# Eight modulation rows moved ahead of the routing, and a new order for the last expert group, in an attention and mixture-of-experts layer

## The reference, cut to what matters

```
mod = silu(c) @ w_ada + b_ada                     # 2048 x 12288, six parts: sh1 sc1 g1 sh2 sc2 g2
h = rmsnorm(x, norm1_g) * (1 + sc1) + sh1;  qkv = h @ w_qkv
y = two attentions (sliding window, blockwise), each normalised;  x = x + g1 * (y @ w_o)
h = rmsnorm(x, norm2_g) * (1 + sc2) + sh2
gates = routing(h)                                # group by softmax, two experts of eight in it
for e in range(32):                               # w_gate, w_up: 2048 x 512;  w_down: 512 x 2048
    out += gates[:, e] * ((silu(h @ w_gate[e]) * (h @ w_up[e])) @ w_down[e])
x = x + g2 * out;  return rmsnorm(x, final_g)     # 256 tokens of 2048
```

## Time and profile before

| | |
|---|---|
| median of 3 runs | 1431.66 us (1430.23 to 1432.35) |
| the profiled execution | 1430.98 us, its span 1429.1 us |
| PE | 1311.6 us busy, 92% |
| DVE | 681.7 us, 48% |
| ACT, POOL | 158.0 us, 62.1 us |
| read from memory | 566.27 MB, 398 GB/s over the span |

### The profile page before, as it was taken

The page is one execution under the profiler, slowest core; times in us unless marked ns, Lnnn a source line. Parts: engine busy times, 40 slices in busy tenths (PEclk is TensorE's granted clock), DMA queues, the critical chain, the costliest instruction groups (busy, mean ns, idle before and its releaser), DMA issues.

```text
span 1429.1 us, 14957 instructions
## 1 busy us (share of the span) xinstructions
PE 1311.6 (92%) x5797; PEld 663.2 (46%) x5797; DVE 681.7 (48%) x1069; ACT 158.0 (11%) x424; POOL 62.1 (4%) x74
## 2 busy tenths in 40 slices
PE   4999999999999999999997998989899799888896
PEld 4686688577888635333332332333233233223332
DVE  5678788699987621432332331333233232232235
ACT  3300000295001302000000000000000000000002
POOL 1000000013000100000000000000000000000000
PEclk9999999999999999999999999999999999999999
DMA  9999999983999999999999999999999999999995
GB/s 337 394 396 387 399 401 392 392 287 117 397 400 422 354 426 425 425 425 423 427 427 427 425 425 427 423 430 425 425 427 427 427 425 425 428 425 428 423 425 206
DMA packets 102961, 569.11 MB, mean 398 GB/s; under 512 B 5216, under 2 KB 19808, under 8 KB 70272
## 3 DMA queue, kind: packets, MB, share of 16 engines
q1 hardware_dynamic: 102384, 567.67, 97.5%
q0 software_dynamic: 528, 0.78, 0.4%
HBM read 566.27 MB, written 2.16 MB: 398 GB/s over the span
## 4 chain that ended last, share of the span: by engine, by line
PE 68%; DMA 26%; DVE 2%; ACT 2%; issue 1%; SPq 1%; DVEq 0%; ACTq 0%
DMA ring<-in_w_up 25%; PE PS L1731 22%; PE PS L1490 12%; PE PS L1695 8%; PE PS L1784 6%; PE PS L1596 6%; PE PS L1493 4%; PE PS L1568 2%; DMA ring<-in_w_ada 1%; PE PS L1678 1%; PE PS L1657 1%; PE PS L1716 1%; PE PS L1517 1%; PE PS L1431 0%; PE PS L1746 0%
## 5 line engine op out<-in xcount | busy, mean ns | idle before, releaser
L1731 PE MATMUL PS<-ring,gysq 128*64 128x512 f32 x960 | 222.7, 619 | 40.6 <-DMA ring<-in_w_up 40.6
L1731 PE MATMUL PS<-ring,W 128*64 128x512 f32 x1024 | 236.7, 620 | 21.4 <-DMA ring<-in_w_up 21.4
L939 DVE SCALAR_TENSOR_TENSOR W<-ring,sm,W 128x1024 f32<-128x1024 f32 (+1 forms) x195 | 234.4, 1202 | 21.7 <-DMA ring<-in_w_ada 5.7
L1784 PE MATMUL PS<-ring,W 128*64 128x512 f32 x992 | 219.7, 595 | 12.4 <-ACT W L864 12.4
L1267 DVE TENSOR_TENSOR r<-r,PS 128x512 f32<-128x512 f32 x120 | 82.5, 687 | 232.2 <-PE PS L1695 232.2
L1490 PE MATMUL PS<-r,ring 128*128 128x256 f32 x768 | 167.2, 379 | 0.7 <-DVE r L978 0.7
L1731 PEld LDWEIGHTS PS<-ring,gysq 128*64 128x64 f32 x960 | 79.3, 143 | 183.2 <-issue 183.2
L1490 PEld LDWEIGHTS PS<-r,ring 128*128 128x128 f32 x768 | 145.7, 190 | 22.9 <-issue 3.4
L1731 PEld LDWEIGHTS PS<-ring,W 128*64 128x64 f32 x1024 | 76.6, 142 | 170.2 <-issue 170.2
L1272 DVE TENSOR_SCALAR W<-W 128x256 f32<-128x256 f32 x32 | 21.0, 658 | 280.4 <-ACT W L860 279.6
L1784 PEld LDWEIGHTS PS<-ring,W 128*64 128x64 f32 x992 | 69.4, 137 | 142.3 <-issue 134.4
(11 more groups left out here) (273 smaller groups left out, 833.7 us busy)
## 6 DMA issues: line engine op xcount, KB each, us to landing
ring<-in_w_gate SPq DMA_DIRECT2D x64, 2048.0 KB, 25.5
ring<-in_w_up SPq DMA_DIRECT2D x64, 2048.0 KB, 28.0
ring<-in_w_down SPq DMA_DIRECT2D x64, 2048.0 KB, 28.4
ring<-in_w_ada SPq DMA_DIRECT2D x32, 2048.0 KB, 18.1
ring<-in_w_ada SPq DMA_DIRECT2D x32, 1024.0 KB, 16.2
ring<-in_w_qkv SPq DMA_DIRECT2D x9, 2048.0 KB, 19.0
ring<-in_w_o SPq DMA_DIRECT2D x8, 2048.0 KB, 17.6
ring<-in_w_qkv SPq DMA_DIRECT2D x8, 1536.0 KB, 16.9
```

Source lines behind the costliest of these rows:

```text
L939: ins = V.scalar_tensor_tensor(total, w, cT[:, t:t + 1], total, ALU.mult, ALU.add)
L1731: last = mm(PS[64 * j:64 * j + 64, i % 2, :].rearrange("p (m n) -> p m n", m=2), hE[i % 2][:, k], w[:, :, t, 256 * j:256 * j + 256], start ...
L1784: last = mm(PS[64 * q:64 * q + 64, bank + i2, :], hidT[:, b, 64 * j:64 * j + 64], w[:, b, 512 * ch:512 * ch + 512], start=(j + b == 0), st ...
```

## The change

Three things are changed together.

- The last two chunks of M7 are loaded right after its first two, before any expert chunk, so that all expert chunks m = 0 to 7 stand in eight different slots. The eight last rows on DVE go into WO_ROWS, which now adds up to 64: one more before residual(4), (6), (8), (10) and (12), and three before residual(15).
- The last group of experts has an order of its own, LAST_GROUP: down of expert 1 comes before gate and up of expert 2. On PE the first scatter follows down(1); between the halves of gate_up(3) stand hid_transpose(2) and six keep_warm products; hid_transpose(3) stands between the chunks of down(2), and its result goes to a buffer of its own (hidT_last).
- The last expert's down weights come in four pieces of 512 columns (1 MB each), each with its own signal. All four pieces are multiplied into partitions 64 to 127, one after the other, each into its own bank, and scaled by one DVE instruction each. The last scatter goes through the first token half and then through the second, and ACT computes the first half's root before the last square.

```diff
-TAIL = [(0, 0), (0, 1), (1, 0), (1, 1), (0, 2), (0, 3), (1, 2), (1, 3)]
+LAST_GROUP = ([(0, k) for k in range(4)] + [(1, k) for k in range(4)] + [(0, 4), (0, 5), (1, 4), (1, 5)]
+              + [(2, k) for k in range(4)] + [(3, k) for k in range(4)] + [(2, 4), (2, 5), (3, 4), (3, 5)])
+LAST_GU_AT = [LAST_GROUP.index((i, 0)) for i in range(4)]
+LAST_DN_AT = [LAST_GROUP.index((i, 4)) for i in range(4)]
+TAIL = [(h, ch) for h in range(2) for ch in range(4)]
 TAIL_BANK = [6, 7, 4, 5]
...
+    rows(LAST, 2, 3)
     first = sum(o[2] is not None for o in order) % RING
-    for k in (2, 3):
-        order.append(("rows", (LAST, k), (first + 4 + k) % RING, "rows", ROW_NO[LAST, 4 * k + 3]))
...
+        hidT_last = idr[:, :].rearrange("p (b n) -> p b n", b=2)
...
-        WO_ROWS = [[2, 2, 2, 2], [12, 2, 1, 1], [12, 2, 1, 1], [14, 1, 1, 0]]
+        WO_ROWS = [[2, 2, 2, 2], [13, 2, 2, 1], [13, 2, 2, 1], [15, 1, 1, 3]]
...
+            def last_down(ch, s):
+
+                n0 = D * (ch % 2)
+                return (slot(s)[:, n0:n0 + D].rearrange("p (t n) -> p t n", n=512), down_v[E - 1, :, :, 512 * ch:512 * ch + 512])
...
-                i, k = GROUP[m % 24]
+                i, k = (GROUP if m < EXP_CHUNKS * E - 24 else LAST_GROUP)[m % 24]
                 e = 4 * (m // 24) + i
                 if e == E - 1 and k >= 4:
-                    dst, src = last_down(k - 4, (S0 + m) % RING)
+                    dst, src = last_down(2 * (k - 4), (S0 + m) % RING)
+                    sp.dma_start(dst, src).then_inc(piece_in[k - 4], 16)
+                    dst, src = last_down(2 * (k - 4) + 1, (S0 + m) % RING)
                 else:
                     dst, src = expert_chunk(e, k, (S0 + m) % RING)
...
-                if (kind, i) == ("rows", (LAST, 2)):
-                    for m in range(6):
-                        expert_load(m)
...
-            for m in range(6, EXP_CHUNKS * E):
+            for m in range(EXP_CHUNKS * E):
                 expert_load(m)
...
-                    free = GU_END[i - 2] if i > 1 else GU_END[i + 2] - 24
+                    free = GU_END[i - 2] if i > 1 else max(GU_END[i + 2], LAST_GU_AT[i + 2] + 4) - 24
...
+                if tail:
+                    hidT_evac(1)
+                    exp_gate(2)
+                    selT_evac(2 * q + 1)
+                    hidT_evac(2)
+                    exp_gate(3)
+                    hidT_evac(3)
+                    return
...
-            last_root(0)
+                if k == 6:
+                    last_root(0)
             last_root(1)
...
+            def last_result(ch):
+
+                if ch % 2 == 0:
+                    dve.wait_ge(piece_ps, ch // 2 + 1)
+                else:
+                    dve.wait_ge(pe_chunk, PE0 + EXP_CHUNKS * E - 1 + ch // 2)
+                n0 = 512 * ch
+                V.tensor_tensor(yd[64:128, n0:n0 + 512], PS[64:128, ch, :], g2b[64:128, n0:n0 + 512],
+                                ALU.mult).then_inc(yd_ok, 1)
...
-            for _ in range(8):
-                row()
...
-                silu_up(q, 2)
-                result(q, 1)
+                if not tail:
+                    silu_up(q, 2)
+                result(q, 1, tail)
                 acc_add(2 * q)
+                if tail:
+                    silu_up(q, 2)
...
                 if tail:
-                    last_result(0)
-                    last_result(1)
+                    for ch in range(4):
+                        last_result(ch)
...
-                dve.wait_ge(f_ms, (6, 8)[h])
+                dve.wait_ge(f_ms, 4 * h + 4)
...
-                for j in range(2):
-                    w = slot(chunk_at(g, DN_AT[3] + j)).rearrange("p (b n) -> p b n", b=4)
-                    for b in range(4):
-                        for q in range(2):
-                            last = mm(PS[64 * q:64 * q + 64, j, :], hidT[:, b % 2, 64 * (b // 2):64 * (b // 2) + 64],
-                                      w[:, b, 512 * q:512 * q + 512], start=(b == 0), stop=(b == 3))
-                    last.then_inc(pe_chunk, 1)
                 p = 2 * g + 1
                 pe.wait_ge(selT_ok, p + 1)
+                for ch in range(4):
+                    if ch % 2 == 0:
+                        s = (S0 + LAST_DN_AT[3] + ch // 2) % RING
+                        pe.wait_ge(piece_in[ch // 2], 16)
+                    else:
+                        s = chunk_at(g, LAST_DN_AT[3] + ch // 2)
+                    w = slot(s)[:, D * (ch % 2):D * (ch % 2) + D].rearrange("p (b n) -> p b n", b=4)
+                    for b in range(4):
+                        last = mm(PS[64:128, ch, :], hidT_last[:, b % 2, 64 * (b // 2):64 * (b // 2) + 64], w[:, b],
+                                  start=(b == 0), stop=(b == 3))
+                    last.then_inc((piece_ps, pe_chunk)[ch % 2], 1)
                 for k, (h, ch) in enumerate(TAIL):
-                    if k % 4 == 0:
-                        pe.wait_ge(yd_ok, 4 * p + 4 + k // 2)
+                    if k < 4:
+                        pe.wait_ge(yd_ok, 4 * p + 3 + k)
...
+                        if j == 0 and between:
+                            between()
 
                 pe.wait_ge(sel_ok, 2 * n + 2)
                 sel_transpose(2 * g, 0)
                 gate_up(g, 1)
                 hid_transpose(0)
                 down(0)
+                if tail:
+                    hid_transpose(1)
+                    down(1)
+                    scatter(2 * g, more)
+                    gate_up(g, 2, tail=True)
+                    sel_transpose(2 * g + 1, 1)
+
+                    def third_transpose():
+                        hid_transpose(2)
+                        keep_warm(4, 6)
+
+                    gate_up(g, 3, third_transpose, tail=True)
+                    down(2, lambda: hid_transpose(3))
+                    last_expert()
+                    return
...
-                if tail:
-                    first_scatter()
-                    gate_up(g, 3)
-                else:
-                    gate_up(g, 3, first_scatter)
+                gate_up(g, 3, first_scatter)
```

More of the change, by code:

```diff
@@ L392, in layer_kernel @@
         landed = [sem(f"landed{s}") for s in range(RING)]
+        piece_in, piece_ps = [sem(f"piece_in{i}") for i in range(2)], sem("piece_ps")
         upper_in, late_in = sem("upper_in"), sem("late_in")
@@ L852, in selT_evac, with expert_group @@
                 A.activation(selT, PS[:, 2, 0:T], ACT.Copy).then_inc(selT_ok, 1)
-            def expert_group(q, rest=False):
+            def expert_group(q, rest=False, tail=False):
                 def exp_gate(i):
-                    act.wait_ge(pe_chunk, PE0 + 24 * q + GU_END[i])
+                    act.wait_ge(pe_chunk, PE0 + 24 * q + (LAST_GU_AT[i] + 4 if tail else GU_END[i]))
                     if i:
@@ L863, in hidT_evac @@
                     act.wait_ge(hd_ps, 4 * q + i + 1)
-                    A.activation(hidT, PS[:, 3, 0:T].rearrange("p (b n) -> p b n", b=2), ACT.Copy).then_inc(hidT_ok, 1)
+                    A.activation(hidT_last if tail and i == 3 else hidT, PS[:, 3, 0:T].rearrange("p (b n) -> p b n", b=2),
+                                 ACT.Copy).then_inc(hidT_ok, 1)
                 exp_gate(0)
@@ L882, in _ @@
             expert_group(0, rest=True)
-            with act.Fori(1, E // 4) as g:
+            with act.Fori(1, E // 4 - 1) as g:
                 expert_group(g)
+            expert_group(E // 4 - 1, tail=True)
             act.wait_ge(routed, 1)
@@ L1280, in silu_up, with result @@
                 V.tensor_tensor(hid, ex, PS[:, i % 2, T:2 * T], ALU.mult).then_inc(hid_ok, 1)
-            def result(g, i):
-                dve.wait_ge(pe_chunk, PE0 + 24 * g + DN_END[i])
+            def result(g, i, tail=False):
+                dve.wait_ge(pe_chunk, PE0 + 24 * g + (LAST_DN_AT[i] + 2 if tail else DN_END[i]))
                 bank = 2 if i == 3 else 4
@@ L1719, in first_gate_up, with gate_up @@
                     last.then_inc(pe_chunk, 2)
-            def gate_up(g, i, between=None):
+            def gate_up(g, i, between=None, tail=False):
+                at = (LAST_GU_AT if tail else GU_AT)[i]
                 pe.wait_ge(win_ok, 4 * g + i + 1)
                 for half in range(2):
-                    s = chunk_at(g, GU_AT[i] + 2 * half)
-                    chunk_at(g, GU_AT[i] + 2 * half + 1)
+                    s = chunk_at(g, at + 2 * half)
+                    chunk_at(g, at + 2 * half + 1)
                     w = ring[:, s * SLOT:(s + 2) * SLOT].rearrange("p (m t n) -> p m t n", m=2, n=FE)
@@ L1767, in hid_transpose, with down @@
                     last.then_inc(hd_ps, 1)
-                def down(i):
+                def down(i, between=None):
                     pe.wait_ge(hidT_ok, 4 * g + i + 1)
@@ L1778, in down @@
                     for j in range(2):
-                        w = slot(chunk_at(g, DN_AT[i] + j)).rearrange("p (b n) -> p b n", b=2)
```

(5 more changed lines are left out.)

7 lines of the change are left out of this document (removed).

## The result

| | |
|---|---|
| before, median of 6 runs | 1430.95 us (1428.41 to 1434.96) |
| after, median of 6 runs | 1445.32 us (1443.92 to 1445.75) |
| ratio | 1.0098, 95% interval 1.0083 to 1.0113 |
| the profiled execution after | 1445.45 us, its span 1443.6 us |

What follows compares the result with a forecast made beforehand. In most of the kernel the stream of weights was taken to set the pace. 1429.1 + 5.4 + 6.9 = 1441.4 us of span; 1.9 to the execution and 0.7 to the median made 1444, range 1437 to 1448.

Steps and rivals of the forecast that it cites:

- The second part: Last group of experts, new order and single pieces: +6.9 us, from -0.2 to +8.5.
- the first part: DVE's rows ahead of the routing make the routing and everything after it late: +5.4 us, from +0.9 to +6.9.
- Where DVE would be: DVE before the routing: rows wait for their chunks, residual(12) at 452.95, 4.95 late, residual(15) at 464.8.
- The rival in which the data come in time: Modulation rows before the routing: earlier reading frees slots earlier, only +0.9, 1439.5 us; chance 0.07.
- PE's clock ahead of the routing: Before the router: PE stands still about 4 us; 1.5 added only to the upper bound, 6.9.
- The hole in the stream: Weight stream at 482 to 484: not closed but moved to between about 493 and 499, longer, its size not counting.
- everything is shifted by 5.4: From the load of m = 26 on: all comes 5.4 us late, no later stretch having slack in the stream.
- The tail: Last group: down(1) waits for result(0), scatter 9.2, six keep_warm products 2.6; last scatter ends +7.4, earlier root gives 0.5.
- The pieces: Last expert's down products, all in partitions 64 to 127: without a partner 0.44 each, 32 instructions take 14.2 us.
- single pieces at the pair's rate: Last expert's down products: pieces run at the pair's rate, end moves by -0.2, 1437 us; chance 0.10.
- The clock falls more often: Pauses before down(1), the scatter and the router: each further fall costs up to 2 us, 1447; chance 0.11.
- The stream gets faster: All chunks: other slots and packets, 4.83 us a chunk in place of 4.90, 1431 or less; chance 0.07.

Runs made afterwards that it cites:

- the first experiment: Kernel before with the new load order and the eight DVE rows ahead of the routing, old tail: 1438.64 us against 1430.54, ratio 1.0054.
- the second experiment: Kernel after with the load order, WO_ROWS and eight late rows of the kernel before, so only the new tail: 1436.64 us, ratio 1.0046.
- its version with pairs: Against the second experiment, last down weights in two chunks of 1024 columns, multiplied into both partition halves by turns: 1430.16 us against 1430.64, ratio 0.9993.

## Why the prediction was right, and where it was off

The forecast was 1444 (1437 to 1448); it measured 1445.3. The second part cost about what was worked out (6.1 for 6.9), the first more (8.1 for 5.4). The total came closer than the first part, and that is partly luck: the clock added 3.7 at the routing, and 1.5 of the lateness went again at a place that the change does not touch. By its steps:

**Where DVE would be: right.** M6 row 8 was to wait for a landing at 422.6 and residual(9) to come at 424.0: 422.82 and 424.03. M7 row 0 at 438.2: 438.45. residual(12) at 452.95: 453.52. residual(15) at 464.8: 465.15, 5.7 late against 5.4, and 5.2 without the 0.55 that were there ahead of the edits. The rival in which the data come in time is out: DVE waited 3.74 and 2.33 for them.

**PE's clock ahead of the routing: the mis-sized term.** The prediction saw that PE would stand still for about 4 us, allowed "1.5" for the clock as an upper bound, and put nothing into the sum. In the kernel after, lateness grew from 5.7 at residual(15) to 9.4 at the issue of m = 8, 3.7 more; in the first experiment from 7.3 to 9.9, 2.6 more. With PE kept busy and the clock at 1.00 only the 1.6 of the extra products was left. So the lower clock cost 2.6 to 3.7, and this is the term that was put at nothing. Its bound was taken from one scatter at the earlier trace rows, which lost 2.1; in the kernel after, the clock was low from about 464.3 to 474.5, under small products and transposes in series for which everything after waits, and in the first experiment it fell twice. Of the 2.6 there, about 1.7 were lost in the second fall, at the idle products and the gather. Under Part 1 of its page TensorE: Matmul & The Clock Gate, the Trainium skill says that the clock is given back after sustained activity. In this trace PE's busy time was 2.00 of 2 in every stretch from 466 to 474, and the clock stayed at 0.50 in them.

**The hole in the stream: right in kind.** Closed at 482, open again from 492 until m = 8 is issued (predicted from 493 to 499), and of no account by itself: the order of the loads alone changed nothing. The lateness passed undiminished through 584.05 (9.4) to the first landing that PE waits for, 642.76 before (9.4):

```profile
652.13 23.64 DMA ring<-in_w_up
```

By the last group's first gate_up it was 9.0, and in its second half more went: before, that half took 8.56 at a clock of 0.52 to 0.63,

```profile
1306.48 8.56 PE PS L1731 x32
```

and after, the one at 1315.48 took 7.09 at 1.00. That leaves 7.5. Nothing shows this as an effect of the change: the same half took 7.09 in the second experiment too, and 8.77 in its version with pairs, which is the same up to there. The prediction's "everything is shifted by 5.4" held in kind. The first part alone cost 8.1 in its median; in its profiled execution the 5.3 of the rows and the clock's 2.6 make 7.9. The prediction's upper bound for it, 6.9, was too low.

**The tail: right in its sum, with two terms that cancel.** The wait before down(1) was there, 1.82 and the 0.4 of a transpose. Down(1) took 8.78 and not 7.1, the scatter 7.67 and not 9.2: the fall came at the first of the two pauses and was over by the scatter.

```profile
1356.00:1358.00 2.00, 2.00 (x7) 0.61 (x5) 0.00 (x0) 0.00 (x0) 0.00 (x0) 0.50 0.96 410
```

From down(1)'s start to the scatter's end 18.8 were predicted and 19.07 measured. The six keep_warm products took 2.59 (2.6). The sum to the last scatter is 7.3 late (7.4), the end gives 0.4 back (0.5 for the earlier root, which was not tested by itself). In the median the second part cost 6.1.

**The pieces: right.** 14.2 was predicted from a scatter product at full width, 13.73 was measured, 0.43 each, and 6.87 as pairs. The rival of "single pieces at the pair's rate" is out. The pairs bring the median down by 6.5 us, and the tail had cost 6.1. At 512 columns an output of 64 partitions takes as long as one of 128 (0.43 and 0.44) unless another stands in the other half. Under Performance Considerations of TensorEngine Tiling (Array Packing), the Trainium skill calls this column tiling; the factor of up to 2 that the page gives under Theoretical Speedup is 2.00 here. The drain at a change of tiling mode, which the prediction weighed, does not show: at the change from the pieces (13.73) to the scatter (6.22) the chain runs without a gap.

**The clock falls more often:** this rival's price, 3 us in all and a time of 1447, is near what came, but from other places. Two of its three pauses lie in the tail; there the one fall cost no more than the sum already had with its scatter of 9.2. The third, before the router, took 3.7 alone, at a price of up to 2 in the rival.

**The stream gets faster:** out. In slices 18 to 38 it stands at 423 to 431 as before, and the order alone measured 0.9993.

**Open.** The profiled executions are apart by up to 3.1 us at SP's issue of 344.38 (343.31 to 346.42), where the kernels are still the same; what sets this is not shown. Nor is it shown why one and the same pause is followed by a lower clock in some executions and not in others, as ahead of 1306.48. And with three rows ahead of residual(15), m = 8 was 4.1 late (3.4 of its own) in the profiled execution, whose time was 1434.58, while the median of 12 runs was 1432.00: whether the clock falls in only some of them was not shown.

## What to carry to other kernels

Work that fills an idle engine is free only as far as its gaps reach: add up what is placed into one gap, with the landing of the data it needs, before each share is called free. Before work is put where another engine has to wait for it, look at what that engine does next: small products and transposes in series, at half the clock, added 2.6 to 3.7 us here to a wait of 5.2. And a matrix product with 64 output partitions should have a partner in the other half: without one the last expert's pieces took twice the time. Pieces that can start earlier are worth nothing when PE is the one that is late.

## What the runs showed that was not expected

- After 4 us with PE nearly still, the granted clock was 0.50 from 466 to 474 although PE was busy for all of it (8 to 12 instructions in 2 us, most of them transposes).
- With only the three rows added ahead of residual(15), where PE was still busy for 1.19 of the 2 us from 460 to 462, the clock fell to 0.50 as well.
- With eight products of 128x256 in the pause it was 1.00 in every stretch from 460 to 502.
- The same half of gate_up, in kernels that are the same up to there, took 7.09 us in one profiled execution and 8.77 in another, after pauses of 2.70 us in both.
